# First attention of a two-block layer stack: the second query product, the value product, the compressed scores and the gates stand at other places among the sliding steps

## The reference, cut to what matters

```python
q, kc, vc, ks, vs, kw, vw, g, qm = split_cols(x @ a_w_in[i], A_IN_SIZES)
k_cmp = nsa_compress(heads(kc), ...)        # gelu(blocks @ w1) @ w2, 15 blocks of 32 rows
v_cmp = nsa_compress(heads(vc), ...)
gates = jax.nn.sigmoid(g).reshape(B, S, N_HEADS, 3)
...
p_c = masked_softmax(q . k_cmp * scale + bias, dist_c >= 0)     # compressed
p_s = masked_softmax(q . ks * scale + bias_s, dist_s >= 0)      # selected blocks
p_w = masked_softmax(q . kw * scale + bias_w, mask_w)           # window
o = gc[..., 0:1] * o_c + gc[..., 1:2] * o_s + gc[..., 2:3] * o_w
...
o_mem = memory_attention(qm, mem, w_mem_kv)
mix = jnp.concatenate([o_main, o_mem], axis=-1) @ w_out
x = layer_norm(ALPHA * x + mix, ...)
```

## Time and profile before

| what | value |
|---|---|
| time, median of 3 runs | 1327.61 us (1326.9 to 1333.41) |
| profiled execution: its own time | 1328.08 us |
| profiled execution: span of the trace | 1326.0 us |
| mean granted TensorE clock, share of full speed | 0.95 |
| TensorE busy | 1168.5 us (88%) |
| VectorE, ScalarE, GpSimd busy | 469.4, 261.1, 332.3 us |

### The profile page before, as it was taken

How to read it: one execution, slowest core, us unless ns; L and a number is a source line. 1 busy time by engine, 2 the same in 40 slices (tenths; PEclk the granted TensorE clock), 3 DMA queues, 4 the chain that set the end, 5 groups by cost and what they waited for, 6 DMA issues and landing times.

```text
span 1326.0 us, 18928 instructions
## 1 busy us (share of the span) xinstructions
PE 1168.5 (88%) x7731; PEld 765.8 (58%) x7731; DVE 469.4 (35%) x1189; ACT 261.1 (20%) x663; POOL 332.3 (25%) x358
## 2 busy tenths in 40 slices
PE   7999899878656666657999999999999999999997
PEld 6855555434312122122576679997468666999843
DVE  4433632010101011010227664444762225444467
ACT  4324430100000000000334522111023222211101
POOL 6000100000000000000102359887001113987800
PEclk9999999998878887887999999999999999999999
DMA  9662658999999999999995046543541067654400
GB/s 351 210 219 89 268 214 352 417 429 423 429 427 427 429 429 430 428 426 422 390 312 191 1 133 218 190 169 118 191 172 50 1 208 236 223 161 157 159 0 32
DMA packets 101375, 335.85 MB, mean 253 GB/s; under 512 B 6745, under 2 KB 58257, under 8 KB 87086
## 3 DMA queue, kind: packets, MB, share of 16 engines
q1 hardware_dynamic: 98678, 326.33, 63.9%
q0 software_dynamic: 2416, 8.30, 1.7%
q10 hardware_dynamic: 199, 0.06, 0.0%
HBM read 333.59 MB, written 2.86 MB: 254 GB/s over the span
## 4 chain that ended last, share of the span: by engine, by line
PE 71%; DMA 18%; DVE 3%; POOL 3%; ACT 2%; issue 1%; SPq 1%; DVEq 0%; ACTq 0%; POOLq 0%
PE bank L1811 19%; PE bank L935 16%; DMA ring<-in_w_expert_up 11%; PE bank L1861 8%; PE bank L1337 5%; PE bank L1355 3%; DMA ring<-in_w_expert_down 2%; DMA ring<-in_w_expert_gate 2%; DMA wide_rows<-in_w_expert_gate 2%; PE bank L1969 2%; PE bank L1224 2%; PE bank L1782 2%; PE bank L1620 2%; PE bank L1593 1%; PE bank L1060 1%
## 5 line engine op out<-in xcount | busy, mean ns | idle before, releaser
L1811 PE MATMUL bank<-R,arena 128*128 128x128 f32 x1056 | 125.1, 275 | 0.0
L1337 PE MATMUL bank<-ring,arena 128*32 128x512 f32 x512 | 77.8, 697 | 51.1 <-DMA ring<-in_w_expert_up 39.6
L1811 PEld LDWEIGHTS bank<-R,arena 128*128 128x128 f32 x1056 | 121.5, 192 | 0.0
L3377 POOL COPY arena<-w_router 128x256 f32<-128x256 f32 x1 | 0.4, 396 | 468.9 <-PE bank L1337 468.9
L2841 DVE TENSOR_TENSOR arena<-arena,bank 64x512 f32<-64x512 f32 x16 | 11.1, 691 | 296.4 <-ACT arena L2220 296.4
L1337 PE MATMUL bank<-wide_rows,arena 128*32 128x512 f32 x128 | 68.1, 684 | 50.2 <-DMA arena<-in_w_expert_up 38.6
L935 PE MATMUL bank<-wide_rows,ring 128*128 128x256 f32 (+1 forms) x464 | 104.9, 384 | 0.0
L935 PEld LDWEIGHTS bank<-wide_rows,ring 128*128 128x128 f32 x464 | 86.9, 190 | 14.3 <-issue 2.1
L1811 PE MATMUL bank<-wide_rows,ring 128*128 128x128 f32 x704 | 91.2, 275 | 1.5 <-ACT wide_rows L2205 1.5
L1811 PEld LDWEIGHTS bank<-wide_rows,ring 128*128 128x128 f32 x704 | 84.7, 192 | 2.5 <-ACT wide_rows L2205 2.5
L1861 PE MATMUL bank<-arena 128*128 128x512 f32 x176 | 81.4, 593 | 0.5 <-DVE arena L3224 0.5
(11 more groups left out here) (434 smaller groups left out, 1964.9 us busy)
## 6 DMA issues: line engine op xcount, KB each, us to landing
ring<-in_w_expert_down SPq DMA_DIRECT2D x29, 2048.0 KB, 16.1
ring<-in_ffn_w_in SPq DMA_DIRECT2D x44, 1024.0 KB, 8.2
ring<-in_w_expert_gate SPq DMA_DIRECT2D x16, 2048.0 KB, 25.8
ring<-in_w_expert_up SPq DMA_DIRECT2D x16, 2048.0 KB, 33.4
arena<-in_w_expert_up SPq DMA_DIRECT2D x14, 2048.0 KB, 32.6
ring<-in_ffn_w_out SPq DMA_DIRECT2D x10, 2048.0 KB, 7.7
arena<-in_w_expert_gate SPq DMA_DIRECT2D x7, 2048.0 KB, 27.0
ring<-in_w_in SPq DMA_DIRECT2D x6, 2048.0 KB, 17.8
```

What stands on the lines that cost most here:

```text
L1337: last = pe.matmul(bank[e % 2][at:at + SLOTS, :], xg_tile(e % 2, k)[:, SLOTS * r:SLOTS * r + SLOTS], w[r][:, kk, :], start=k == 0, stop=k ...
L1811: last = pe.matmul(up_banks[layer][u % 4][i][:, at * P:(at + 1) * P], weights(k), columns(k), start=k == 0, stop=k == KT // 2 - 1)
```

## The change

The list `first_attention` is written in another order, and two entries of `last_job` are changed to fit it. `a_q` 1 moves from ahead of step 2 to behind `cmp_h`; `a_q` 2 and `cmp_l` move behind step 5; `a_v` keeps its place between steps 4 and 5; `gates` moves behind step 6 and `cmp_pT` behind step 7. No instruction is added or removed.

```diff
     return [("a_qm", 0), ("a_kv", 0), ("step", 0), ("a_q", 0), ("step", 1), ("a_q", 1), ("step", 2), ("cmp_h", 0),
-            ("a_q", 2), ("cmp_hT", 0), ("step", 3), ("cmp_kv", 0), ("a_kv", 1), ("cmp_l", 0), ("step", 4), ("a_v", 0), ("step", 5), ("gates", 0),
-            ("step", 6), ("cmp_pT", 0)] + [("step", i) for i in range(7, 20)] + [("last", 0)]
+    return [("a_qm", 0), ("a_kv", 0), ("step", 0), ("a_q", 0), ("step", 1), ("step", 2), ("cmp_h", 0), ("a_q", 1), ("cmp_hT", 0),
+            ("step", 3), ("cmp_kv", 0), ("a_kv", 1), ("step", 4), ("a_v", 0), ("step", 5), ("a_q", 2), ("cmp_l", 0), ("step", 6),
+            ("gates", 0), ("step", 7), ("cmp_pT", 0)] + [("step", i) for i in range(8, 20)] + [("last", 0)]
...
-            last_job = {("free", 1): ("a_kv", 1), ("free", 2): ("a_v", 0), ("free", 4): ("cmp_h", 0),
+            last_job = {("free", 1): ("a_q", 2), ("free", 2): ("a_v", 0), ("free", 4): ("cmp_h", 0),
...
-            for c, job in ((0, ("a_q", 1)), (1, ("a_kv", 1)), (2, ("a_v", 0))):
+            for c, job in ((0, ("a_q", 1)), (1, ("a_q", 2)), (2, ("a_v", 0))):
```

More of the change, by code:

```diff
@@ L196, in first_attention @@
 def first_attention():
-    return [("a_qm", 0), ("a_kv", 0), ("step", 0), ("a_q", 0), ("step", 1), ("a_q", 1), ("step", 2), ("cmp_h", 0),
-            ("a_q", 2), ("cmp_hT", 0), ("step", 3), ("cmp_kv", 0), ("a_kv", 1), ("cmp_l", 0), ("step", 4), ("a_v", 0), ("step", 5), ("gates", 0),
-            ("step", 6), ("cmp_pT", 0)] + [("step", i) for i in range(7, 20)] + [("last", 0)]
+    return [("a_qm", 0), ("a_kv", 0), ("step", 0), ("a_q", 0), ("step", 1), ("step", 2), ("cmp_h", 0), ("a_q", 1), ("cmp_hT", 0),
+            ("step", 3), ("cmp_kv", 0), ("a_kv", 1), ("step", 4), ("a_v", 0), ("step", 5), ("a_q", 2), ("cmp_l", 0), ("step", 6),
+            ("gates", 0), ("step", 7), ("cmp_pT", 0)] + [("step", i) for i in range(8, 20)] + [("last", 0)]
 def between_turnings():
```

## The result

The changed kernel takes 1339.72 us (median of 6 runs, 1338.42 to 1343.01), the kernel before 1330.29 beside it (6 runs, 1326.4 to 1333.41). The ratio is 1.0078, 95% interval 1.006 to 1.0096. The profiled execution takes 1339.44 (span 1337.3), 11.36 more than the one of before.

What follows compares the result with a forecast made beforehand. The prediction took TensorE, busy 88% of the span, as the bound. Waits of 10.9 us less 2.7 for the holes that go, plus 1.7 of clock, gave +9.9 us: 1337.5 us, range 1333.5 to 1340.5.

Steps and rivals of the forecast that it cites:

- A: Ahead of `cmp_h`, moved before `a_q` 1: TensorE waits 6.2 us for the second compression weight to land.
- B: Step 4's scores, directly behind `a_kv` 1: TensorE waits 1.1 us for ScalarE's copy of the keys.
- C: `cmp_l` directly behind `a_q` 2: TensorE waits 0.65 us for ScalarE's copy of `a_q` 2.
- D: Step 7's transposes: TensorE waits 0.95 us for ScalarE's copy, queued behind the exponent of the compressed scores.
- E: Step 7's scores: TensorE waits 1.8 us until VectorE has finished the compressed shares and read set 6's scores.
- F: Ahead of `cmp_pT`: TensorE waits 0.2 us for VectorE's gated shares, estimated between nothing and 0.5.
- the queues: DMA issue and GpSimd's list in the new order: loads still arrive in time, GpSimd mostly idle, so no cost.
- Clock at A: Behind the wait for the compression weights: TensorE's clock falls to half, costing 1.7 us, between nothing and 2.6.
- Clock in the late part: Behind the waits of step 7: a clock loss of 1.6 us, cancelling the 1.6 lost before.
- the old holes: Three TensorE idle times in step 6 of the kernel before, 1.11, 1.31 and 0.25 us; these 2.7 go away.

Runs made afterwards that it cites:

- the first half alone: Kernel before with only `a_q` 1 moved behind `cmp_h` and joined to `a_q` 2; 1336.28 us, ratio 1.0044.
- the second execution: The changed kernel profiled once more, unaltered; its stage took 126.64 us against 130.00 at first.
- the late part alone: Kernel before with `a_q` 2 and `cmp_l` behind step 5, `gates` and `cmp_pT` as in the change, all ahead of `cmp_h` as before; 1332.94 us, ratio 1.0023.
- the kernel awake everywhere: Changed kernel with products of zeros in the wait for the compression weights, around `cmp_l` and in step 7; 1337.17 us, ratio 1.0055.
- The kernels kept awake: Kernels with added products of zeros: the kernel awake everywhere, 1337.17 us, and the kernel before with zeros in step 6 and `cmp_l`, 1327.83 us.
- the kernel with the gates early: The kernel awake everywhere with `gates` moved ahead of step 6; 1336.7 us, ratio 1.0071.
- the kernel before, kept awake in step 6: Kernel before with eight products of zeros, four ahead of step 6's scores and four ahead of its values; 1328.26 us, ratio 0.9986.

## Why the prediction was right, and where it wasn't

Direction held, and so did the mechanism of waits A to E. The time, 1339.72 us, lies inside 1333.5 to 1340.5, but the small miss is partly luck. The kernel before has its median at 1330.29 here and not at 1327.61, so the medians differ by 9.43 where 9.9 was forecast; and the stage grew by 11.42 in the first pair of executions and by 8.14 in the second (126.64 - 118.50), with errors of both signs in it. Step by step:

- **A, 6.2:** 4.81 + 0.93 = 5.74, ended by the named transfer. It was sized against a step 2 that runs through; step 2's own 0.93 wait lay inside it. With the clock behind it, this is 7.9 of the 11.4; the first half alone, 8.7, bears that out. In the second execution it is 4.48: A moves by 1.3 us with the landing, more than the half microsecond allowed.
- **B 1.1, C 0.65:** 1.10 and 0.73.
- **D 0.95, E 1.8:** 0.43 and 1.40, less because TensorE arrived later, at half clock. In the second execution D is nothing and E 1.45. VectorE's part was sized rightly: its readings end 5.1 us behind `cmp_l` (722.88 in the chain, `cmp_l`'s end at 717.78), against 5.15.
- **F, 0.2: the step that failed.** From these readings to `cmp_pT` I gave 1.9 us, TensorE's 1.7 and the wait. It took 3.44 (722.88 to 726.32). I took L3008 at 0.56 from the earlier trace rows, and wrote of the queues that GpSimd's list "is unchanged" and these "cost nothing". Moved behind step 6 the product met GpSimd's wide set and took 1.40, and the L3046 ahead of it 1.03. So `cmp_pT` came 8.5 us behind `cmp_l` where the terms of D, E and F add up to 7.05 (1.8 + 0.95 + 0.6 + 1.8 + 1.7 + 0.2). As a wait F is 1.57 or 1.58 in the second execution, in the late part alone and in the kernel awake everywhere. The 0.17 of the first execution is no hit: half-clock TensorE came late and hid the rest.
- **Clock at A, 1.7:** 2.2 (38.57 - 36.34) in the first execution and 1.3 in the second, within its bounds. The rule of the Trainium skill ("TensorE: Matmul & The Clock Gate", section "HAM oscillation — how this bites in real kernels") agrees: the clock was back at 0.50 behind the wait for a DMA.
- **Clock in the late part, nothing on balance:** wrong in its place and its reason. I called waits D and E "the old holes once more in other places", with a clock loss that "cancels what is lost before". The fall begins at `cmp_l`, ahead of both. In the rows it cost 3.64 against 1.66 before in the first execution, and in the second 0.43 + 0.52 + 0.46 + 0.16 = 1.57 (step 6 and the transposes of step 7) against 0.66 + 0.46 + 0.46 = 1.58 (`cmp_pT` and step 7). On the path it cost less than before, where the chain runs through TensorE from `cmp_pT` on and the whole loss counts: 1.28 against 1.66 in the first, and in the second nothing, since the clock was up again by 721.3, ahead of `cmp_pT`. The kernels kept awake agree for the first: 64.82 - 64.01 and 0.4 for the zeros is 1.2, and 118.58 - 117.37 and 0.4 is 1.6. So the clock made up for a part of F, and in the second execution a shorter A did so too.

Open: why the clock falls at `cmp_l` in some executions. Behind `a_q` 2, with 0.73 us of waiting ahead, it fell in all six runs without zeros there, and with zeros in one of two (down in the kernel with the gates early, up in the one without). In its old place it fell in one of the four runs that have it there unfilled. The runs don't settle which of its narrow products, the wait, or chance decides.

## What to carry to other kernels

A projection that seems out of place in a hand-written order may be the cover of a transfer or of a copy: before moving it, list what it hides (here 7.1 us over a landing that only just comes in, 6.4 us over a softmax) and what stands there instead. A product that is moved to another engine neighbour can change its length, so read what the other engines run at its new place (here 0.56 us became 1.40). Products at half clock cost time only where the chain runs through them. And where total times scatter by more than the effect, the length of the stage shows what the total can't.

## What the runs showed of the hardware

- In the kernel before, kept awake in step 6, the granted clock fell to 0.50 behind 24 products of 32 columns in a stretch that the rows show busy throughout (window 702 to 703 at 1.00 busy, 703 to 704 at a clock of 0.58). I had looked for it behind idle times only.
- One and the same order had a half-clock stretch of 10.2 us behind `cmp_l` in one execution and of 3.4 in the next.
- VectorE's product with two inputs in SBUF took 1.40 us beside GpSimd's and 0.56 away from them; a two-column one took 1.02 for 0.16.
- In the changed order, VectorE's part from `cmp_l` to `cmp_pT` took 8.54 to 8.56 us whether TensorE ran beside it at 0.50 or at 1.00.
